# Moving the small steps of two recurrent mixers into the dense tiles before them, and spreads written as transposes

## What is computed

```
prev = jnp.pad(hb, ((0, 0), (1, 0), (0, 0)))[:, :-1]
hb = hb + (prev - hb) * mu                               # shift
r, k, v, wd, ad, gd = split_cols(hb, RWKV_SPLITS)
w_log = -jax.nn.softplus(-(w0 + jnp.tanh(wd) @ w_up)) - 0.5   # decay gate
a = jax.nn.sigmoid(a0 + ad @ a_up)
g = jax.nn.sigmoid(gd) @ g_up
kk = l2_normalize(heads(k * k_k), 1e-12)                 # the recurrent keys' norm
```

## Time and profile before

| | |
|---|---|
| runs of the kernel before | 3562.01, 3560.09, 3561.99 us; median 3561.99 |
| the profiled execution | 3561.09 us, span 3559.3 us, mean granted PE clock 0.977 |
| PE busy | 3407.8 us (96% of the span) |
| DVE, ACT, POOL busy | 1420.2, 1254.9, 1657.9 us (40%, 35%, 47%) |
| from the first head spread of layer 0 to its first 512-key item on DVE | 510.19 to 587.03 us |
| the same in layer 1 | 1694.90 to 1771.74 us |

### The profile page before, as it was taken

The page is one execution under the profiler, slowest core; times in us unless marked ns, Lnnn a source line. Parts: engine busy times, 40 slices in busy tenths (PEclk is TensorE's granted clock), DMA queues, the critical chain, the costliest instruction groups (busy, mean ns, idle before and its releaser), DMA issues.

```text
span 3559.3 us, 47689 instructions
## 1 busy us (share of the span) xinstructions
PE 3407.8 (96%) x17100; PEld 2804.4 (79%) x17100; DVE 1420.2 (40%) x2753; ACT 1254.9 (35%) x1890; POOL 1657.9 (47%) x2052
## 2 busy tenths in 40 slices
PE   7999998799999999999878999999899999999999
PEld 6888775688888888887658888888767888888887
DVE  5431487855221332137787432214563110341100
ACT  4222335434222422233463332223533332333321
POOL 6765542005665566554300266644403555535554
PEclk9999998899999999999889999999999999999999
DMA  5443321003443344333100144432202222213222
GB/s 182 146 143 106 110 86 48 13 4 116 145 144 118 118 149 146 118 103 98 60 25 1 60 147 142 136 101 88 77 1 72 94 100 94 77 65 101 94 95 100
DMA packets 104225, 340.52 MB, mean 96 GB/s; under 512 B 12144, under 2 KB 17936, under 8 KB 103968
## 3 DMA queue, kind: packets, MB, share of 16 engines
q1 hardware_dynamic: 83984, 277.83, 23.5%
q10 hardware_dynamic: 20112, 60.89, 5.3%
HBM read 330.78 MB, written 2.65 MB: 94 GB/s over the span
## 4 chain that ended last, share of the span: by engine, by line
issue 43%; POOL 33%; PE 23%; POOLq 0%; DVE 0%; ACT 0%; DVEq 0%
POOL w_lo L663 33%; PE ps L2204 7%; PE ps L2206 7%; PE ps L2205 7%; PE ps L3058 0%; PE ps L2227 0%; PE ps L2228 0%; PE ps L2232 0%; PE ps L3064 0%; POOLq L660 0%; PE ps L3013 0%; PE ps L3015 0%; PE ps L3014 0%; POOLq L671 0%; PE ps L3062 0%
## 5 line engine op out<-in xcount | busy, mean ns | idle before, releaser
L663 POOL TENSOR_TENSOR w_lo<-w_raw,w_hi 128x256 fp32r<-128x256 f32 x2040 | 1651.3, 841 | 1884.1 <-ACT w_hi L706 1877.9
L2204 PE MATMUL ps<-h_hi,w_hi 128*128 128x512 f32 x2608 | 1020.3, 391 | 1.4 <-ACT mem L934 1.4
L2206 PE MATMUL ps<-h_hi,w_lo 128*128 128x512 f32 x2608 | 1015.8, 389 | 0.0
L2205 PE MATMUL ps<-h_lo,w_hi 128*128 128x512 f32 x2608 | 1015.3, 389 | 0.0
L706 ACT ACTIVATE w_hi<-w_raw 128x1024 fp32r<-128x1024 f32 x510 | 538.3, 1057 | 904.0 <-DMA w_raw<-in_tiles 903.7
L2204 PEld LDWEIGHTS ps<-h_hi,w_hi 128*128 128x128 f32 x2608 | 489.9, 188 | 114.2 <-ACT mem L932 5.6
L2206 PEld LDWEIGHTS ps<-h_hi,w_lo 128*128 128x128 f32 x2608 | 489.8, 188 | 102.8
L2205 PEld LDWEIGHTS ps<-h_lo,w_hi 128*128 128x128 f32 x2608 | 490.1, 188 | 100.8
L2205 PE MATMUL ps<-a_lo,w_hi 128*128 (+1 forms) x1120 | 435.8, 389 | 0.0
L2204 PE MATMUL ps<-a_hi,w_hi 128*128 (+1 forms) x1056 | 410.8, 389 | 0.0
L2206 PE MATMUL ps<-a_hi,w_lo 128*128 (+1 forms) x1056 | 410.8, 389 | 0.0
(11 more groups left out here) (473 smaller groups left out, 3666.6 us busy)
## 6 DMA issues: line engine op xcount, KB each, us to landing
w_raw<-in_tiles SPq DMA_DIRECT2D x510, 512.0 KB, 3.3
ada_raw<-in_ada_tiles ACTq DMA_DIRECT2D x96, 512.0 KB, 3.3
mem<-mem ACTq DMA_DIRECT2D x80, 64.0 KB, 2.0
x<-in_x_t SPq DMA_DIRECT2D x2, 1024.0 KB, 6.4
sq<-in_cond ACTq DMA_DIRECT2D x4, 512.0 KB, 3.8
mem<-gates SPq DMA_DIRECT2D x8, 256.0 KB, 4.1
consts<-in_consts SPq DMA_DIRECT2D x1, 1280.0 KB, 12.8
core_mem<-gates SPq DMA_DIRECT2D x8, 128.0 KB, 3.0
```

Source lines behind the costliest of these rows:

```text
L663: ins = nc.gpsimd.tensor_tensor(w_lo[:, s, part], w_raw[:, s, part], w_hi[:, s, part].bitcast(F32), ALU.subtract)
L2204: nc.tensor.matmul(bank, wh, hi, start=first, stop=False, skip_group_check=True)
L2205: nc.tensor.matmul(bank, wh, lo, start=False, stop=False, skip_group_check=True)
L2206: return nc.tensor.matmul(bank, wl, hi, start=False, stop=last, skip_group_check=True)
```

## The change

- **Gates.** The six low-rank products go into recurrent tile 12, after the third of its eight blocks; ACT's gates follow its copy of tile 11. PE no longer waits for them between the tiles and the items. Tanh and Sigmoid stand before ACT's copy of tile 11 instead of 13.
- **Spreads.** The five head spreads have a bank each (2, 3, 4, 5, 7) and stand after tiles 6, 6, 7, 7 and 8, with no wait for DVE. Every `head_spread` and `spread_rstd` is now made of transposes instead of matmuls with the identity.
- **Shift.** DVE does it in pieces between the heads' scalings, before the last 20 rounds of `best_keys`, and the unnormed keys and their factor right after it.
- **Cumulative sums, keys' norm.** DVE's cumulative sums and the keys' inverse norm follow the top keys, ahead of DVE's wait for the last tile. PE sums the keys' squares after tile 13, waiting for `gates_ready` and the squares. ACT takes the root and the decay's exponentials after copying tile 13, waiting for DVE's `decay_in`, with its copy of tile 14 queued behind.
- **Softplus.** DVE's three steps stand at the start of the attention tiles (with the masks in layer 0), ACT's Exp and Ln after it has rounded a tile at `m` = 5, ahead of the DMAs of `swap_halves`.

Cut to its core (leading blanks shortened):

```diff
+        SPREAD_BANKS = (2, 3, 4, 5, 7)
+        SPREADS_AT = {6: (0, 1), 7: (2, 3), 8: (4,)}
+        LORA_TILE = 12
+        U_KK, U_KK_SQ, U_SOFT = 29, 31, 38
...
+            if m == 5:
+                early = mem[ROW_A:ROW_A + 4, U_SOFT, :]
+                act.wait_ge(S["sp_in"], l + 1)
+                link(nc.scalar.activation(early, early, ACT.Exp))
+                nc.scalar.activation(early, early, ACT.Ln, bias=eps(EPS_ONE)[ROW_A:ROW_A + 4, :]).then_inc(S["sp_ln"], 1)
...
-            if m == REC_TILES - 2:
+            if m == LORA_TILE - 1:
 
                 lg = rw[:, 6, 1:T + 1]
                 act.wait_ge(S["shifted"], l + 1)
                 nc.scalar.activation(lg[0:32, :], lg[0:32, :], ACT.Tanh)
                 nc.scalar.activation(lg[64:128, :], lg[64:128, :], ACT.Sigmoid).then_inc(S["lora_in"], 1)
+                act.wait_ge(S["kk_in"], l + 1)
+                nc.scalar.activation(mem[:, U_KK_SQ:U_KK_SQ + 2, :], mem[:, U_KK:U_KK + 2, :], ACT.Square).then_inc(S["head_sq"], 1)
...
-        act.wait_ge(S["lora_ready"], l + 1)
-        for c in range(2):
-            nc.scalar.activation(mem[:, c, :], ps[:, 2 + c, :], ACT.Sigmoid, bias=param(f"w0{l}", c))
-            nc.scalar.activation(mem[:, 2 + c, :], ps[:, 4 + c, :], ACT.Sigmoid, bias=param(f"a0{l}", c))
-            ins = nc.scalar.activation(mem[:, 43 + c, :], ps[:, 6 + c, :], ACT.Copy)
-        ins.then_inc(S["gates_ready"], 1)
-
-        beta = mem[ROW_B:ROW_B + 4, U_MISC, :]
-        nc.scalar.activation(beta, beta, ACT.Sigmoid).then_inc(S["beta_ready"], 1)
-
-        def meanwhile(i):
-
-            if i == 1:
-                act.wait_ge(S["kk_in"], l + 1)
-                nc.scalar.activation(core_mem[:, R_SQ:R_SQ + 2, :], core_mem[:, R_KK:R_KK + 2, :], ACT.Square).then_inc(S["head_sq"], 1)
...
+            if m == LORA_TILE - 1:
+                act.wait_ge(S["lora_ready"], l + 1)
+                for c in range(2):
+                    nc.scalar.activation(mem[:, c, :], ps[:, 2 + c, :], ACT.Sigmoid, bias=param(f"w0{l}", c))
+                    nc.scalar.activation(mem[:, 2 + c, :], ps[:, 4 + c, :], ACT.Sigmoid, bias=param(f"a0{l}", c))
+                    ins = nc.scalar.activation(mem[:, 43 + c, :], ps[:, 6 + c, :], ACT.Copy)
+                ins.then_inc(S["gates_ready"], 1)
+                beta = mem[ROW_B:ROW_B + 4, U_MISC, :]
+                nc.scalar.activation(beta, beta, ACT.Sigmoid).then_inc(S["beta_ready"], 1)
+            if m == LORA_TILE + 1:
+                head_roots(7, 2, 1.0, EPS_L2)
                 act.wait_ge(S["decay_in"], l + 1)
...
-            if i == 4:
-                head_roots(0, 2, 1.0, EPS_L2)
...
-            if i == 7:
-                act.wait_ge(S["sp_in"], l + 1)
-                link(nc.scalar.activation(soft, soft, ACT.Exp))
-                nc.scalar.activation(soft, soft, ACT.Ln, bias=eps(EPS_ONE)[ROW_A:ROW_A + 4, :]).then_inc(S["sp_ln"], 1)
...
+        dve.wait_ge(S["raw_evened"], l + 1)
+        s, early = (mem[ROW_A:ROW_A + 4, u, :] for u in (U_MISC, U_SOFT))
+        link(nc.vector.tensor_scalar(s, s, param(f"dt{l}")[ROW_A:ROW_A + 4, :], None, ALU.add))
+        link(nc.vector.scalar_tensor_tensor(early, s, -1.0, s, ALU.mult, ALU.min))
+        nc.vector.tensor_scalar(s, s, 0.0, None, ALU.max).then_inc(S["sp_in"], 1)
+        if l == 0:
+            derive_masks()
...
-            if p >= 4:
+            if 4 <= p < len(INDEX_PAIRS) - 1:
...
+        scale_heads((0, 1))
+        dve.wait_ge(S["proj_out"], first + ATT_TILES + 7)
+        V.tensor_tensor(mem[:, 2:6, :], rw[:, 0:4, 0:T], rw[:, 0:4, 1:T + 1], ALU.subtract)
+        link(V.tensor_tensor(steps, rw[:, 4:7, 0:T], rw[:, 4:7, 1:T + 1], ALU.subtract))
+        shift(range(2))
+        scale_heads((2, 3))
+        shift(range(2, 4))
+        scale_heads((4,))
+        shift(range(4, 7)).then_inc(S["shifted"], 1)
+        dve.wait_ge(S["shifted"], l + 1)
+        kk_raw = mem[:, U_KK:U_KK + 2, :]
+        for c in range(2):
+            V.tensor_scalar(kk_raw[:, c, :], rw[:, 2 + c, 1:T + 1], param(f"k_k{l}", c), None, ALU.mult)
+            ins = V.tensor_scalar(stat[:, ST_OMKA + c:ST_OMKA + c + 1], param(f"k_a{l}", c), -1.0, 1.0, ALU.mult, ALU.add)
+        ins.then_inc(S["kk_in"], 1)
+        best_keys(2, range(12, 16))
+        best_keys(1, range(16))
+        dve.wait_ge(S["sp_in"], l + 1)
+        dve.wait_ge(S["sp_ln"], l + 1)
+        link(V.tensor_tensor(s, s, early, ALU.add))
...
+        dve.wait_ge(S["gates_ready"], l + 1)
+        for c in range(2):
+            for n in range(TB):
+                ins = V.tensor_tensor_scan(mem[:, 4 + c, blk(n)], const("ones"), mem[:, c, blk(n)], 0.0, ALU.mult, ALU.add)
+        link(ins)
+        cum = by_block(mem[:, 4:6, :])
+        mid, end, gam = block_columns(ST_CM), block_columns(ST_CE), block_columns(ST_GAMMA)
+        V.tensor_copy(mid, cum[:, :, :, HD - 1])
+        link(V.tensor_copy(end, cum[:, :, :, P - 1]))
+        link(V.tensor_tensor(gam, end, mid, ALU.subtract))
+        V.tensor_tensor(gam[:, :, 0:TB - 1], gam[:, :, 0:TB - 1], mid[:, :, 1:TB], ALU.add)
+        link(V.tensor_tensor(cum, cum, mid.unsqueeze(3).to_broadcast([P, 2, TB, P]), ALU.subtract))
+        V.tensor_tensor(mem[:, 0:2, :], mem[:, 4:6, :], mem[:, 0:2, :], ALU.subtract).then_inc(S["decay_in"], 1)
+        head_inverse(mem[:, U_KK_SQ:U_KK_SQ + 2, :], 2)
...
-            if i == 1 and l == 0:
-                derive_masks()
-            if i == 2:
-
-                dve.wait_ge(S["gates_ready"], l + 1)
...
-            if i == 6:
-                head_inverse(core_mem[:, R_SQ:R_SQ + 2, :], 2)
...
-            if i == 3:
-                link(V.tensor_scalar(s, s, param(f"dt{l}")[ROW_A:ROW_A + 4, :], None, ALU.add))
-            if i == 4:
-                link(V.scalar_tensor_tensor(soft, s, -1.0, s, ALU.mult, ALU.min))
-            if i == 5:
-                V.tensor_scalar(s, s, 0.0, None, ALU.max).then_inc(S["sp_in"], 1)
             if i == 10:
-                dve.wait_ge(S["sp_ln"], l + 1)
-                link(V.tensor_tensor(s, s, soft, ALU.add))
...
-            if between and k == KD - 2:
+            if between and k == after:
...
-            ins = nc.tensor.matmul(ps[:, 7, j * P:(j + 1) * P], rtok[:, j:j + 1].to_broadcast([P, P]), const("ident"), start=True, stop=True)
+            ins = nc.tensor.transpose(ps[:, 7, j * P:(j + 1) * P], rtok[:, j:j + 1].to_broadcast([P, P]), const("ident"))
...
-            ins = nc.tensor.matmul(ps[:, bank, blk(n)], chunk[:, blk(n)], const("ident"), start=True, stop=True)
+            ins = nc.tensor.transpose(ps[:, bank, blk(n)], chunk[:, blk(n)], const("ident"))
...
+        def lora_products():
+
+            pe.wait_ge(S["lora_in"], l + 1)
+            pe.wait_ge(S["v_out"], l + 1)
+            pe.wait_ge(S["head_done"], due("head_done", 5))
+            lg = rw[:, 6, 1:T + 1]
+            for c in range(2):
+                for bank, rows in ((2, slice(0, 32)), (4, slice(32, 64)), (6, slice(64, 128))):
+                    ins = nc.tensor.matmul(ps[:, bank + c, :], lora[rows, l, blk(c)], lg[rows, :], start=True, stop=True)
+            ins.then_inc(S["lora_ready"], 1)
+
         for m in range(REC_TILES):
             pe.wait_ge(S["proj_out"], first + m - 1)
-            linear_tile(ps[:, m % 2, :], base + m)
+            linear_tile(ps[:, m % 2, :], base + m, between=lora_products if m == LORA_TILE else None, after=2)
...
-            if 6 <= m < 11:
-                if m >= 8:
-
-                    pe.wait_ge(S["head_done"], head0 + m - 7)
-                head_spread(mem[:, 33 + m - 6, :], 4 + m % 2).then_inc(S["head_spread"], 1)
+            for s in SPREADS_AT.get(m, ()):
+                if s == 4:
+                    pe.wait_ge(S["v_out"], l + 1)
+                head_spread(mem[:, 33 + s, :], SPREAD_BANKS[s]).then_inc(S["head_spread"], 1)
+            if m == LORA_TILE + 1:
+                pe.wait_ge(S["gates_ready"], l + 1)
+                pe.wait_ge(S["head_sq"], due("head_sq"))
+                head_sums(mem_units(U_KK_SQ, U_KK_SQ + 1), 7).then_inc(S["head_sum"], 1)
         due("proj_out", REC_TILES)
         due("roped", 5)
-        pe.wait_ge(S["head_done"], due("head_done", 5))
-
-        pe.wait_ge(S["lora_in"], l + 1)
-        pe.wait_ge(S["v_out"], l + 1)
-        lg = rw[:, 6, 1:T + 1]
-        for bank, rows in ((2, slice(0, 32)), (4, slice(32, 64)), (6, slice(64, 128))):
-            for c in range(2):
-                ins = nc.tensor.matmul(ps[:, bank + c, :], lora[rows, l, blk(c)], lg[rows, :], start=True, stop=True)
-        ins.then_inc(S["lora_ready"], 1)
-        pe.wait_ge(S["gates_ready"], l + 1)
...
-            if i == 2:
-                pe.wait_ge(S["head_sq"], due("head_sq"))
-                head_sums(squares_of_keys, 0).then_inc(S["head_sum"], 1)
```

55 lines of the change are left out of this document (15 added, 40 removed).

## The result

| | before | after |
|---|---|---|
| median of six runs, us | 3561.12 | 3539.14 |
| lowest and highest run | 3559.98, 3564.40 | 3536.79, 3549.52 |
| the profiled execution, its span | 3561.09, 3559.3 | 3536.79, 3535.0 |

The changed kernel takes 0.9942 of the time before, with a 95% interval of 0.9931 to 0.9953: 20.6 us less, 16.7 to 24.6 (22.0 between the two medians).

A forecast was written before the change was run, and what follows sets the result against it. PE, busy 96% of the span, was taken as the bound; -21.0 (items), +2.0 (tile 5), -1.4 (items' end), -3.0 (`post`), -4.0 (norms) made -27.4, from 3561.1 to 3533.7, median 3534.6 us, range 3525 to 3549.

The forecast's parts named there:

- rival A: Tiles end later: DVE's path 3 us slower or tile 5's 3.9 us fully paid; 3 us per layer, 3540.6; 20%.
- Dense tiles: PE's tiles before the items: transposed spreads 0.53 us each, 0.9 us wait in tile 12, tile 14 ending at 563.3.
- DVE to `decay_in`: DVE from the shift through top-key rounds, softplus' sum, masks and cumulative sums: `decay_in` at 562 to 563.3 us.
- ACT's chain as the new bound: ACT at the tiles' end sets the items' start: tile 14's copy at 565.4, first exponential at 567.8 us.
- Items 0 to 7: Little stands between the first items, so DVE takes the first 512-key maximum at 577.2 instead of 587.03: -9.8 us.
- Tile 5: Softplus on ACT at attention tile 5 makes PE 1.0 us late per layer: +2.0, bounds 0 to 3.9 per layer.
- `post`: Two pairs of spreads per layer become half as long in PE's gapless stream: 1.5 us taken per layer, -3.0.
- B: The clock comes back later, two pairs of items per layer at 1.2 GHz: 9.4 us lost, 3544; 15%.
- E: The clock does not fall at all before the items: 3 us less per layer, 3528.6; 9%.
- C: All twelve later pairs of items at 1.2 GHz: 28 us more per layer, 3591, slower than before; 3%.
- D: Something unmoved, such as a transfer, paces the later items, so the early start is given back: about 3560; 3%.
- signs of being wrong: PE waits over 2 us at attention tiles 6-8 or tile 12, DVE's items after 567, PEclk 0.50 past first 512-key items.

The follow-up runs named there:

- e9: The changed kernel unedited, run again beside the kernel before: median 3540.2 us, ratio 0.9939.
- e8: The changed kernel with cumulative sums, root, inverse norm and decay's exponentials put back among the first items: 3554.4 us.
- e6: e1 with ACT's root ahead of tile 13's rounding and its next rounding behind the first two exponentials: 3535.3 us.
- e11: e5 with ACT's root ahead of tile 13's rounding and its last two roundings behind the exponentials of items 9 and 11: 3531.9 us.
- e1: The changed kernel with softplus' Exp and Ln moved from attention tile 5 to after the rounding at recurrent tile 8: 3533.3 us.
- e4: The changed kernel with only the spreads of `post` made as matmul products again: 3540.6 us.
- e5: e1 with the gates' products after the fifth block of tile 12 instead of the third: 3528.9 us.
- e10: e5 plus 9 and 6 matmuls that nobody reads, in PE's waits at the first items: 3523.3 us.
- e7: e1 plus 9 and 6 matmuls that nobody reads, in PE's waits at the first items: 3531.3 us.

## Why the prediction was right, and where it was not

The time lies 4.5 us above the forecast of 3534.6 and inside the range; faster was right. It is nearer to rival A's 3540.6, and half of A is what happened. By its steps:

- **Dense tiles.** Right. PE was to end tile 14 at 563.3; it ended at 565.5 having started 2.2 late. The wait in tile 12 was to be 0.9 us (0.80 and 1.35), the keys' sums 1.8 (1.84), a transposed spread 0.53 (about 0.5 in the stream). The gates' products cost the stream 4.4 us and not 3.85, which tiles of 5.44 us instead of 5.49 and other small differences made up for. What was missing is that the wait in tile 12 can bring the clock down, 3 us at a time: the profiled execution had no such fall, e9 had two.
- **DVE to `decay_in`.** 562 to 563.3 forecast, 564.26 measured, that is on time counting from the late start. One duration was wrong: the eight scans took 2.63 us in the earlier trace rows and 4.60 here, because POOL now works beside them (its four pieces at 557.57 take 3.33 us, those at 570.23, with DVE mostly idle, 2.77); in e8, where POOL is idle for nearly all of them, they take 2.63 again. The rounds before them left room. The Trainium skill (SBUF — State Buffer, Who interferes with whom) states that a DVE instruction with two inputs in SBUF contends with a GpSimd one that reads SBUF; these rows agree.
- **ACT's chain as the new bound.** Right, step for step: copy done at 565.4 forecast, at 567.85 measured, of which 2.2 are the late start; the first exponential at 567.8, and at 570.06. Without those 2.2 us all of it is within 0.3. e6 and e11 show that the first exponential does hang on it, and also that little is to be won there.
- **Items 0 to 7.** -9.8 forecast, -10.9 and -10.5 measured. e8 shows the largest part of it directly.
- **Tile 5, the term that was mis-sized.** "Following ACT's queue with its idle gaps I get PE 1.0 us late per layer": up to the first head spread it was 2.5 in layer 0 and 4.0 in layer 1. The wait grew by 1.4 us in layer 0, and the clock fell in it, which costs as much again. In layer 1 tile 5 itself has 2.8 of the 4.0; another 0.9 comes with a wait of 1.01 us for ACT's relu at 1672.99, behind DVE's rounds, which e1 has too and so is not the softplus', and 0.3 with two shorter delays. The bounds of 0 to 3.9 had only the wait in them, not the clock. This was the tile-5 half of rival A, and e1 confirms it.
- **`post`, the other one.** -3.0 forecast, -0.6 measured: the shorter spreads are followed by a fall of the clock (e4). The step that failed is the one that weighed the rule on transposes by the row at 652 to 656 alone. It was not wrong for that row; the same rule was at work in another place, where narrow sums of two columns stand between the spreads and the products.
- **Clock among the items: rivals B and E.** The clock fell (E out) and came back at about 577, within the first 512-key scores, as forecast; in layer 0 it fell again from 584 to 588, after PE had idled 1.54 us, which is B's beginning; DVE is the bound there, and from the first 512-key maximum to the last it takes 45.0 us with this fall and 45.0 without (e5). In layer 1 it did not fall again until 1799.3, 4 us before the last maximum; before it had fallen at such a place too (1819.4, 5 us before). C and D did not happen: 588 to 634 has a grant of 0.98. E's price of 3 us per layer was right in size: e10 gets 2.8 by holding the clock.
- **DVE's masks and softplus ahead of the rotary steps.** Covered, as forecast: the second of these steps starts 0.9 us later than before (414.84, before 413.94), the third 1.0 earlier (418.28, before 419.24).
- **Norms.** 0.45 each forecast; 0.47 from one norm to the next in the stream.
- **Its own signs.** The signs of being right came but for a tenth of a microsecond (65.9 us in layer 0, where 66 to 69 was said; 66.4 in layer 1). But three of the four signs of being wrong came too: a PE wait of over 2 us for ACT behind attention tile 7 (2.59 and 2.24), DVE reaching the items later than 567 (567.88, of which 2.2 are the late start), and a clock of 0.50 beyond the first 512-key items (584 to 588). The first two are the mis-sized tile 5. The third cost nothing that could be seen.

The errors have opposite signs: the items and what follows them brought 4.7 us more than forecast, tile 5, `post` and the norms 7.8 less. The rest of the 4.5 us is that the median lies 2.4 above the profiled execution, where I had taken 0.9. That the total came out so near is in part luck.

## What to carry to other kernels

A wait of one to three microseconds on PE, in a stream that is otherwise dense, is to be priced with the fall of the clock that may follow, here 1.6 to 3 us; and as a chance, since the same wait let the clock fall in some executions only (10 of 16 in tile 12, 6 of 10 at tile 5), and waits of 0.7 to 1.7 us behind attention tile 7 in none of 18. The first place to look for it is the trace before, in every layer: one such fall stood there. A move into "free" time pays where it takes work out of a chain (the sums among the items: 7 us per layer) and costs where the engine's queue has no slack just then (softplus at tile 5); behind the same two functions at recurrent tile 8 no new wait was seen. And a rounding or another feeder's step, moved to where its own engine has time, brings its followers (here POOL's low part) against other work.

## What was not expected of the hardware

- The clock falls in or behind waits far shorter than the 3.9 us that the prediction had read: of 0.6 to 1.7 us in tile 12 (10 of 16 mixers), of 1.8 to 2.6 us at tile 5 (6 of 10), and in `post` behind transposes and narrow sums with a wait of only 0.54 us (14 of 22). Which executions have it I can't say; what decides in one of them is open.
- Nine and six matmuls that nobody reads hold the clock at 1.00 through the first items (e7, e10), at 0.24 us each in time that was idle.
- DVE's scans beside POOL take 1.7 to 2.4 times as long (4.60 for 2.63, 3.23 for 1.36).
